# x's first block loaded by halves, keys' rotation moved behind the normalising, one cast moved to VectorE, in a two-model transformer kernel

## The reference, cut to what matters

```python
def hybrid_layer(x, ...):                     # twice
    h = rmsnorm(x, norm_g)
    proj = h @ w_in                           # 1024 x 8704, split into
    aq, ak, av, az, buv, bz, cq, ck, cv, cz, gl = split_cols(proj)
    # a: differential attention, 4 heads of 2 x 64, causal
    qa, ka = partial_rope(aq), partial_rope(ak)
    oa = (softmax(q1 k1) - lam * softmax(q2 k2)) @ va
    ya = rmsnorm(oa) * (1 - lam_init) * silu(az)
    # b: gated mixing along the tokens
    yb = u * mixed * silu(bz)
    # c: 8 heads of 64, windows with dilation 1, 4, 16, joined by their log-sum-exps
    qc, kc = partial_rope(cq), partial_rope(ck)
    yc = oc * silu(cz)
    merged = sum_n(sigmoid(gl[n]) * (y[n] @ w_branch[n]))
    return x + merged @ w_out
x = hybrid_layer(hybrid_layer(x)); x = rmsnorm(x, final_g)
```

## Time and profile before

| | |
|---|---|
| median of 3 runs | 2322.68 us (2322.1 to 2323.67) |
| the profiled execution's own time | 2325.3 us |
| its span in the profile | 2323.5 us |
| TensorE busy | 2308.4 us (99%) |
| VectorE busy | 1481.2 us (64%) |
| ScalarE busy | 978.6 us (42%) |
| the 16 DMA engines, SP's queue | 30.9% of their time |
| chain that ended last | 96% TensorE, 2% VectorE, 1% ScalarE |

### The profile page before, as it was taken

How to read it: one execution, slowest core, us unless ns; L and a number is a source line. 1 busy time by engine, 2 the same in 40 slices (tenths; PEclk the granted TensorE clock), 3 DMA queues, 4 the chain that set the end, 5 groups by cost and what they waited for, 6 DMA issues and landing times.

```text
span 2323.5 us, 30126 instructions
## 1 busy us (share of the span) xinstructions
PE 2308.4 (99%) x11442; PEld 1881.9 (81%) x11442; DVE 1481.2 (64%) x2781; ACT 978.6 (42%) x1811; POOL 0.2 (0%) x4
## 2 busy tenths in 40 slices
PE   9999999999999999999999999999999999999998
PEld 6888888888888878888877788888887768888887
DVE  6788763435478784444587668566567777658565
ACT  5356542223446553222567543232336764323222
POOL 0000000000000000000000000000000000000000
PEclk9999999999999999999999999999999999999999
DMA  4333334333243333233221133314313112422322
GB/s 167 107 105 105 104 96 112 92 99 100 84 117 109 97 103 114 93 100 117 65 88 55 56 127 102 127 55 145 118 37 97 55 46 100 145 82 91 127 64 99
DMA packets 74766, 226.84 MB, mean 98 GB/s; under 512 B 15296, under 2 KB 16192, under 8 KB 73856
## 3 DMA queue, kind: packets, MB, share of 16 engines
q1 hardware_dynamic: 74336, 224.14, 30.9%
q10 hardware_dynamic: 288, 0.79, 0.1%
HBM read 205.36 MB, written 2.10 MB: 89 GB/s over the span
## 4 chain that ended last, share of the span: by engine, by line
PE 96%; DVE 2%; ACT 1%; issue 0%; DMA 0%; DVEq 0%; SPq 0%
PE bank L590 25%; PE bank L592 25%; PE bank L591 25%; PE bank L2235 2%; PE bank L2237 2%; PE bank L2236 2%; PE bank L1310 2%; PE bank L2054 1%; PE bank L2013 1%; PE bank L1294 1%; PE bank L2038 1%; PE bank L524 1%; PE bank L1283 1%; PE bank L1281 1%; PE bank L2067 1%; PE bank L2096 0%
## 5 line engine op out<-in xcount | busy, mean ns | idle before, releaser
L590 PE MATMUL bank<-h_hi,w_hi 128*128 128x512 f32 x1984 | 784.7, 396 | 0.7 <-DVE sz L1769 0.3
L592 PE MATMUL bank<-h_lo,w_hi 128*128 128x512 f32 x1984 | 773.4, 390 | 0.0
L591 PE MATMUL bank<-h_hi,w_lo 128*128 128x512 f32 x1984 | 773.0, 390 | 0.0
L1157 DVE TENSOR_TENSOR w_lo<-raw_w,w_hi 128x1024 fp32r<-128x1024 f32 x314 | 378.9, 1221 | 97.4 <-ACT w_hi L1145 94.1
L590 PEld LDWEIGHTS bank<-h_hi,w_hi 128*128 128x128 f32 x1984 | 372.7, 188 | 82.5 <-issue 8.3
L592 PEld LDWEIGHTS bank<-h_lo,w_hi 128*128 128x128 f32 x1984 | 372.4, 188 | 79.8
L591 PEld LDWEIGHTS bank<-h_hi,w_lo 128*128 128x128 f32 x1984 | 372.9, 188 | 72.1
L1145 ACT ACTIVATE w_hi<-raw_w 128x1024 fp32r<-128x1024 f32 x314 | 327.6, 1054 | 159.5 <-DMA raw_w<-w_dram 159.1
L2472 ACT ACTIVATE nrm<-bank 128x512 f32<-128x512 f32 x44 | 26.4, 599 | 288.4 <-PE bank L592 288.4
L1611 ACT ACTIVATE ext<-bank 128x512 f32<-128x512 f32 x48 | 28.7, 598 | 274.3 <-PE bank L592 274.3
L1918 DVE TENSOR_TENSOR rope_a<-ext,bank 128x512 f32<-128x512 f32 x32 | 22.0, 688 | 165.8 <-PE bank L592 109.7
(11 more groups left out here) (372 smaller groups left out, 3504.6 us busy)
## 6 DMA issues: line engine op xcount, KB each, us to landing
raw_w<-w_dram SPq DMA_DIRECT2D x312, 512.0 KB, 3.6
down_raw<-w_dram SPq DMA_DIRECT2D x36, 512.0 KB, 4.5
extra_raw<-w_dram SPq DMA_DIRECT2D x10, 512.0 KB, 4.6
k_lo<-k_lo SPq DMA_DIRECT2D x32, 128.0 KB, 2.3
ln_row<-row_dram SPq DMA_DIRECT2D x4, 1024.0 KB, 6.6
last_raw<-w_dram SPq DMA_DIRECT2D x8, 512.0 KB, 4.6
rowp<-row_dram SPq DMA_DIRECT2D x2, 1024.0 KB, 11.9
rot_t<-raw_t SPq DMA_DIRECT2D x128, 16.0 KB
```

Of the source, the lines that this page charges most:

```text
L590: nc.tensor.matmul(dst, lh, rh, start=start, stop=False)
L591: nc.tensor.matmul(dst, ll, rh, start=False, stop=False)
L592: return nc.tensor.matmul(dst, lh, rl, start=False, stop=stop)
L1157: nc.vector.tensor_tensor(lo_of(u), raw_of(u), hi_of(u).bitcast(F32), ALU.subtract) \
```

## The change

It has three parts. The first splits the load of x's block 0: ScalarE's queue loads rows 0 to 63, SP's queue rows 64 to 127, behind `colp` and ahead of weight unit 0, and ScalarE waits for both. The second takes unit 1's cast to its high part from ScalarE (`cast_units[0] = 2` marks it as done) and gives it to VectorE, between h_lo of block 0 and the norm of block 1. The third moves work within VectorE's loop for heads 4, 5 and 6: at query block 2 the epilogue (where there is one, heads 5 and 6) and the normalising now come ahead of the keys' rotation.

```diff
             for tb in range(NB):
-                if tb:
-                    sp.dma_start(x[:, tb, :], x_in[tb * P:(tb + 1) * P, :]).then_inc(x_loaded[tb], 16)
+                rows = slice(0 if tb else HD, P)
+                sp.dma_start(x[rows, tb, :], x_in[tb * P:(tb + 1) * P, :][rows, :]).then_inc(x_loaded[tb], 16)
                 if tb < 2:
                     load(tb)
...
             if layer == 0:
-                act.dma_start(x[:, 0, :], x_in[0:P, :]).then_inc(x_loaded[0], 16)
+                act.dma_start(x[0:HD, 0, :], x_in[0:HD, :]).then_inc(x_loaded[0], 16)
...
             def first_rms(tb):
-                act.wait_ge(x_loaded[tb], 16)
+                act.wait_ge(x_loaded[tb], 16 if tb else 32)
                 rms(st, e, tb)
...
                 first_rms(1)
-                cast_to(act, 1)
+                cast_units[0] = 2
                 entry_hi(act, e, 1, (0,))
...
             split_to(dve, n)
             entry_lo(dve, e, 0, (0,))
+            dve.wait_ge(raw_loaded[TURN[1] % RAW], 16 * loaded_parts(1))
+            nc.vector.tensor_copy(hi_of(1), raw_of(1)).then_inc(hi_cast, 1)
             norm_half(1, 0)
             split_to(dve, n + 1)
...
-                    if second1(a, qb):
+                    if qb == 2 and a in JOINED1 and a > N_A:
+                        dve.wait_ge(y_ready, at(y_ready, 3 + a))
+                        epilogue(a - 1, False)
+                    if qb in (1, 2) and a in JOINED1:
                         normalise(a, qb)
                     if before in ROTATE1:
                         rotate(*ROTATE1[before])
...
                         epilogue(EPILOGUE1[a, qb])
-                    elif qb == (2 if a in JOINED1 else 1) and a > N_A:
+                    elif qb == 1 and a > N_A and a not in JOINED1:
                         epilogue(a - 1, False)
...
-                    if not second1(a, qb):
+                    if qb not in (1, 2) or a not in JOINED1:
                         normalise(a, qb)
```

## The result

The changed kernel takes 2326.57 us (median of 20 runs, 2325.39 to 2328.82), the kernel before 2323.03 (20 runs on the same chip, 2321.45 to 2325.13). The ratio is 1.0014 with an interval of 1.0008 to 1.0019: slower by some 3.5 us. That is inside the 4.6 us that the prediction called no change, yet the interval excludes none at all. The forecast was 2322.2, and its range ended at 2324.2. Of the 21 runs of the kernel before that the later experiments share, one took 13,212 us, in a slow state; it stands in their median, which it hardly moves, and is left out of the ratios.

The account below looks back on a forecast made before the run. TensorE, busy 99% of the span, was taken as the bound, with some 15 us idle to win. The start's -0.7 and the rotation's +0.2 gave -0.5 us, so 2322.2 us was forecast, range 2320.0 to 2324.2.

Parts of the forecast that it names:

- The other joined heads show none: Part 3: TensorE's waits of 1.28 + 0.19 = 1.47 us per layer occur at head 5, none at other joined heads.
- covered by 0.9: Part 3, head 7: keys land at 311.6, scores start at 312.50, so the later keys cost no wait.
- The term: Part 3 over both layers: 2 x 0.1 = +0.2 us, from -2.9 to +4.
- The signs that the prediction had named for itself: L1173 near 4.45, VectorE's cast near 12.9, w_lo's matmul near 15.7, idle moved to head 6's scores, k_lo issues 1.7 later.
- Part 3 in head 5: Both waits, 1.47 us per layer, go; keys come 1.72 later; TensorE waits 1.6 before head 6's scores; net +0.1 per layer.
- The step of the halved queue: Start: q10 runs out 256 KB earlier, 0.7 us at this pace; colp taken 0.6 us earlier, bounds 0 and 1.5.
- The start's sum: Parts 1 and 2 together: -0.7 us, from -1.4 to +0.4.
- If that moment stays: Start: TensorE's clock rises at about 11.8; if fixed, 0.3 of colp's 0.6 us gain goes into dummies.
- The rival that less idle brings the rise forward: Start: TensorE rises to its higher level earlier as the 1.52 us idle shrinks; 1.4 us, 2320.8 us; chance 0.10.
- The keys arrive later still: Landings of 3.7 us delay head 6's scores 1.5 and head 7's 0.6: +3.5, 2326.2 us; chance 0.06, once only 0.14.
- The keys arrive in time: Part 3: transfers overlap the rotation's last part, so 2 x 1.47 = 2.9 us go: 2319.1 us; chance 0.12.
- The start gives little: Start: colp doesn't come earlier, so -0.2 + 0.2 = 0: 2322.7 us; chance 0.16.

Follow-up runs that it names:

- the cover: Kernel before plus part 3 in heads 4 and 5 only, and half a weight tile on TensorE ahead of head 6's joined scores: 2320.88 us, ratio 0.9985.
- the run of parts 1 and 2: Kernel before plus the split load of x's block and unit 1's cast on VectorE, without part 3: 2323.49 us, ratio 0.9997.
- part 3 alone: Kernel before plus only epilogue and normalising ahead of the keys' rotation in heads 4, 5 and 6, start unchanged: 2326.72 us, ratio 1.0013.
- head 6 only: Kernel before plus part 3 in head 6, with heads 4 and 5 in the old order: 2327.32 us, ratio 1.0011.
- the epilogue left behind: Kernel before plus part 3 in heads 4, 5 and 6, but in head 6 only the normalising goes ahead of the rotation: 2331.52 us, ratio 1.0037.
- heads 4 and 5: Kernel before plus part 3 in these two heads, with head 6 in the old order: 2325.33 us, ratio 1.0007.

## Why the prediction was wrong, point by point

**The step that failed** is part 3's "The other joined heads show none" and, resting on it, "Head 7's keys: last issue 307.61 + 1.72 + 2.3 = 311.6, scores at 312.50, covered by 0.9". I looked at what the moved instructions cost in head 6, and not at whether their inputs were ready at the earlier place. They were not. In the profile of before, VectorE ends w_lo in head 6 near 301.6 and goes on to the rotation, while the products that the epilogue reads end at 303.4. The rows of TensorE and of VectorE before, in head 6:

```profile
302.28 1.09 PE L1310 MATMUL bank<-pT,vs 128*64 128x128 f32 x16
```

```profile
301.55 0.68 DVE L1800 TENSOR_TENSOR rope_a<-raw_t,cos 128x512 f32<-128x512 f32 x1
```

With 302.28 + 1.09 - 301.55 = 1.8 us of waiting put in, the sum would have been 307.61 + 1.72 + 1.8 + 2.3 = 313.4 against 312.50, a wait of about 1 us in head 7 in each layer in place of 0.9 us of cover. Measured: idle of 1.09, and 1.28 and 1.26 us lost. The term was +0.2; part 3 measured +2.9 in the profile and by the median. Of the 4.0 us between the forecast change of -0.5 and the measured +3.5, head 6 is 2.5; the start gave 0.4 less than forecast, head 5 cost 0.2 more, and 0.9 stays open (below). The signs that the prediction had named for itself all looked at the start and at head 5, and there they came in kind, the start's at other times; none looked at VectorE in front of head 6's epilogue.

**Part 3 in head 5** was right in each number: both waits gone, k_lo later by 1.72 against w_lo, idle of 1.56 where 1.6 was worked out, landings of 2.35 to 2.4 us where I took 2.3, net +0.19 and +0.17 where I took +0.1. The run with the cover shows that the 2 x 1.47 = 2.9 us are real: they come out as -3.1 once TensorE has other work while the keys travel.

**Part 2** was right: a cast of 0.68 us (0.75 forecast), the 0.20 gone, -0.28 at the matmul.

**Part 1** went its way with another size. colp came 0.27 us earlier and not 0.6. The step of the halved queue, "256 KB earlier, which at this pace is 0.7 us", took x's packets for all that held colp; what else holds it no row shows. That colp does come earlier is safe: L1173 starts at 4.73 to 4.90 in the four kernels with part 1 and at 5.04 to 5.18 in the seven without. x itself came later, which I had not expected at all: its second half landed 4.5 us after its issue, and its statistics start at 6.12 instead of 4.78. The rows of the changed kernel:

```profile
4.78 1.29 DVE L1173 TENSOR_TENSOR gain_diag<-const,colp 128x512 f32<-128x512 f32 x2 [3.39 <-DMA colp<-col_dram]
...
6.12 1.06 ACT L545 ACTIVATE junk<-x 128x1024 f32<-128x1024 f32 x1 [3.52 <-DMA x<-x_dram]
```

The slack of over 2 us hid that, as costed: the norm starts at 8.43, behind gain_row. The rule that the prediction quoted from the Trainium skill (DMA: Bandwidth & Descriptors, Rules for kernel authors), that halves share the engines and bring nothing, is borne out for x, by 1.3 us on the wrong side; the 0.27 us of colp it does not cover.

**The start's sum**, -0.7, was -0.3 by the run of parts 1 and 2, which its interval can't tell from either. Of the 1.52 us by which the two profiles differ at the matmul upon the second w_lo, 0.27 are colp's and 0.28 the cast's. The rest, 1.0, is the moment of the clock's rise, near 10 instead of near 12, which the prediction had taken for a fixed one ("If that moment stays"). A further 0.8 arises up to 70 us in small steps; 0.3 to 0.6 of it is also there in four of the five kernels whose start is that of before (part 3 alone, head 6 only, the cover, the epilogue left behind), and the rest is open. I take both for the spread between executions, since parts 1 and 2 brought 0.3 by the medians; the interval of that run would also allow more. The rival that less idle brings the rise forward is not shown: it came earliest in two kernels with the start of before, whose idle was 1.57 and 1.64 us, and later in the changed one with 1.24.

**The rivals.** *The keys arrive later still* came out to the number, 2326.2 against 2326.57, but by luck and not by its mechanism. It asked for landings of 3.7 us and for 1.5 us lost in head 6; the landings took 2.4, head 6 lost 0.2, and head 7's keys were issued 2 us later than I had it. (Its term for head 7 is 307.61 + 1.72 + 3.7 - 312.50 = 0.53, not 0.6.) I had left the delay of the issue without a range and put all doubt into the landing. *The keys arrive in time* is not what happened, but its price, 2.9, is what the cover brought. *The start gives little* fits the -0.3 of parts 1 and 2 by its number; its reason, that colp would not come earlier, does not hold.

**What stays open.** The changed kernel is 3.5 us above the one before, where the rows explain 2.9 and the start takes back 0.3. The difference of 0.9 is within the interval (+1.9 to +4.4). A fall of the clock behind the new waits, as in the run with heads 4 and 5, would add to it in some executions, but the profile of the changed kernel shows none, so this is not shown. Nor was it tried whether a longer cover ahead of head 7's scores would rescue head 6's part.

## What to carry to other kernels

An instruction that is moved ahead can wait for its own inputs, and then it holds everything that it was moved past. So for each place that an edit touches, also those where the engine shows no wait now, look up when the producer of the moved step's inputs ends and when its output buffer comes free, and set both against the time at which the engine would get there. A wait that is traded for a transfer's latency is only won when the consumer has other work ready for the time of the transfer: the same move brought nothing in head 5 without half a weight tile in between, and 3 us with it.

## What had not been expected of the hardware

- The moment at which TensorE first reaches its higher level (2.4 GHz) differed between executions of code that is the same up to there by nearly 6 us, from just after 6 to near 12, with the engine busy without a gap from 5.9 or 6.0 on to beyond 12 in each. That moves all that follows by up to 2.9 us, beside a spread of 3.7 us over the runs of before (2321.45 to 2325.13). The Trainium skill (TensorE: Matmul & The Clock Gate, Part 1) says that the warm-up varies from run to run, by half a microsecond either way. The rows agree that it varies, but over nearly 6 us, and the measurement decides: a single profile should therefore not be used to price an edit ahead of that moment.
- An idle of 1.59 us, in an engine that was otherwise busy, was followed 1.7 us later by 3 us at the lower level in one execution and by none in another. There the wait of 1.6 us cost 3.1. Behind the start, the profiles have ten waits of 1.5 us and more on TensorE (two in the changed kernel, two with part 3 alone, two with heads 4 and 5, four with the epilogue left behind). Four of them have such a fall behind them, at a cost of 1.5 to 1.6 us each. Between 20 us and the last 6 us of the kernel, where the granted clock drops in every profile, the eleven profiles have no other.
- The second half of a 512 KB block, on SP's queue behind the identity and colp, landed 4.5 us after its issue and later than the whole block had done before.
